# Four edits around norm boundaries, weight slabs and row loads in a six-layer fp32 kernel on one core

## What is computed

```python
for i in range(2):                                  # first block
    h = rms_norm(x, norm_mix[i]);  x = x + (dsa_moba_mixer if i == 0 else nsa_mixer)(h, ...)
    x = x + memory_cross_attention(rms_norm(x, norm_mem[i]), rms_norm(mem, norm_mem_src[i]), ...)
    x = x + swiglu(rms_norm(x, norm_ffn[i]), ffn_w_in[i], ffn_w_out[i])     # 1024 -> 2*2816 -> 1024
for i in range(4):                                  # second block
    mod = silu(c) @ ada_w[i] + ada_b[i];  sh1, sc1, g1, sh2, sc2, g2 = split(mod, 6)
    h = rmsnorm(x, mix_norm_g[i]) * (1 + sc1) + sh1
    x = x + (1 + g1) * mixer_i(h)
    h = rmsnorm(x, ffn_norm_g[i]) * (1 + sc2) + sh2
    x = x + (1 + g2) * conv_ffn(h, ff_w_up[i], ff_conv_w[i], ff_conv_b[i], ff_w_down[i])
return rmsnorm(x, final_g)
```

## Time and profile before

| what | value |
|---|---|
| median of 3 runs (lowest to highest) | 2610.83 us (2610.54 to 2617.75) |
| profiled execution | 2622.73 us |
| its span, first to last instruction | 2620.9 us |
| mean granted TensorE clock | 0.966 of full |
| PE / weight loads / DVE / ACT / POOL busy | 95% / 78% / 56% / 20% / 4% |
| weight stream | 638 slabs of 512 KB; DMA mean 173 GB/s |

### The profile page before, as it was taken

One profiled execution on the slowest core, in us unless ns is written; L12 is line 12 of the kernel. 1 busy time (PEld: TensorE's weight loads), 2 busy tenths in 40 slices (PEclk: granted clock), 3 DMA queues, 4 the chain that ended last, 5 costly groups with the idle time before them and its releaser, 6 DMA issues.

```text
span 2620.9 us, 38049 instructions
## 1 busy us (share of the span) xinstructions
PE 2484.9 (95%) x14704; PEld 2054.0 (78%) x14704; DVE 1472.4 (56%) x3034; ACT 512.1 (20%) x1297; POOL 111.1 (4%) x212
## 2 busy tenths in 40 slices
PE   7898999998898999999999899999999999999997
PEld 4465999755558998689889588898787897689897
DVE  4744787456546885333676445763845674333363
ACT  2221110024311101112211332102222101102210
POOL 0000000000000000000110001100001100000000
PEclk9879999996799999999999999999999999999999
DMA  6123456630125556535776147764227774434432
GB/s 229 67 97 141 154 209 234 217 131 1 37 104 193 209 188 247 177 121 193 281 264 243 71 163 279 279 235 162 103 97 278 283 263 155 174 123 145 152 121 97
DMA packets 122351, 453.30 MB, mean 173 GB/s; under 512 B 13776, under 2 KB 13904, under 8 KB 121680
## 3 DMA queue, kind: packets, MB, share of 16 engines
q1 hardware_dynamic: 92880, 338.24, 35.7%
q0 software_dynamic: 29312, 112.80, 12.2%
HBM read 449.93 MB, written 1.05 MB: 172 GB/s over the span
## 4 chain that ended last, share of the span: by engine, by line
PE 82%; DVE 10%; DMA 3%; ACT 3%; issue 2%; SPq 0%; POOL 0%; DVEq 0%; ACTq 0%
PE pair L517 65%; PE bank L517 16%; DMA ring<-stream_dram 2%; DVE att_s L1596 1%; DVE h L1377 1%; DVE arena L1591 1%; DVE adat L1710 1%; ACT arena L1128 1%; DVE rstd L1374 1%; DVE arena L1473 1%; ACT arena L1140 1%; DMA arena<-gmws_dram 1%; PE bank L739 0%; DMA adat<-adaw_dram 0%; DVE arena L2048 0%
## 5 line engine op out<-in xcount | busy, mean ns | idle before, releaser
L517 PE MATMUL pair<-h,ring 128*128 128x256 f32 (+1 forms) x4352 | 875.8, 363 | 24.6 <-DVE x L1404 6.8
L517 PEld LDWEIGHTS pair<-h,ring 128*128 128x128 f32 x4352 | 772.8, 191 | 123.1 <-DVE arena L1682 9.2
L517 PE MATMUL pair<-arena,ring 128*128 128x128 f32 (+1 forms) x2432 | 386.1, 319 | 12.6 <-DVE x L1404 7.5
L517 PEld LDWEIGHTS pair<-arena,ring 128*128 128x128 f32 x2432 | 352.5, 194 | 43.8 <-DVE x L1404 8.3
L517 PE MATMUL pair<-ring,h 128*128 128x512 f32 (+1 forms) x768 | 325.9, 582 | 3.0 <-DVE h L1377 3.0
L517 PE MATMUL pair<-arena 128*128 128x128 f32 (+6 forms) x2178 | 271.3, 299 | 11.8 <-ACT arena L1119 3.6
L517 PEld LDWEIGHTS pair<-ring,h 128*128 128x128 f32 x768 | 142.5, 191 | 170.6 <-issue 163.8
L517 PEld LDWEIGHTS pair<-arena 128*128 128x128 f32 (+3 forms) x2178 | 229.6, 193 | 47.9 <-issue 25.6
L1710 DVE CUSTOM_DVE_ANT_0 adat<-adat,crow,cols 128x1024 f32<-128x1024 f32 x192 | 244.0, 1277 | 22.1 <-DMA adat<-adaw_dram 21.9
L517 PE MATMUL bank<-arena 128*128 128x128 f32 (+2 forms) x1976 | 239.5, 297 | 14.7 <-ACT arena L1140 7.9
L517 PEld LDWEIGHTS bank<-arena 128*128 128x128 f32 (+2 forms) x1976 | 211.7, 191 | 39.7 <-ACT arena L1140 18.4
(11 more groups left out here) (225 smaller groups left out, 1837.4 us busy)
## 6 DMA issues: line engine op xcount, KB each, us to landing
ring<-stream_dram SPq DMA_DIRECT2D x638, 512.0 KB, 4.4
adat<-adaw_dram POOLq DMA_DIRECT2D x192, 512.0 KB, 4.4
arena<-gmrows_dram POOLq DMA_DIRECT2D x2, 2560.0 KB, 11.2
arena<-cmpw_dram POOLq DMA_DIRECT2D x1, 2112.0 KB, 8.2
x<-x_in_dram SPq DMA_DIRECT2D x2, 512.0 KB, 4.7
arena<-mem_in_dram SPq DMA_DIRECT2D x1, 1024.0 KB, 12.9
arena<-gmws_dram POOLq DMA_DIRECT2D x2, 512.0 KB, 13.2
out_dram<-h POOLq DMA_DIRECT2D x2, 512.0 KB, 3.8
```

The costliest lines, as they stand in the source:

```text
L517: return nc.tensor.matmul(out, lhsT, rhs, start=start, stop=stop)
```

## The change

Four groups of edits, all in the order and the waits; the arithmetic is the same.

1. **Bank waits.** Where `bank_free` waited for the full read of a tail group (both halves), it now waits for the add of its half 0 (`x_half`), because half 1 lies in other banks. `HALF_FREED` maps the counts.
2. **Half 1's sum of squares** moves three half-width products forward in kinds F and S (`late`: n == 0, k == 7 instead of n == 1, k == 2).
3. **DVE order.** The first pair's `up_weights` moves from ahead of `residual("memo…")` to between the last square sum of half 1 and `normalise` of half 1 (`between_halves`). `mem_source(1)` moves into `up_tiles(0)`, ahead of its third pair. The first `down_weights` of `down0` and `down1` moves behind the last gated product and its `moving_sums`.
4. **Slabs and rows.** In the first `down` pair, PE waits for all four weight sums before `one 2` instead of before `two 2`, and gives the pair's slabs back there; before, it gave them back at the start of the second pair. POOL no longer waits for the gMLP rows to land (only before the output), and their second load moves six `ada_w` tiles later.

```diff
+        HALF_FREED = {}
+        for name, source in SOURCE.items():
+            lin = PLAN[source]
+            for n in range(TAIL):
+                HALF_FREED[FREER[lin.g0 + lin.groups - TAIL + n][1]] = TAILS[name] + n + 1
...
-                pool.wait_ge(sem("gm_in"), 32 * (1 + j))
...
-            ada_tiles(ADA_T // 2 + ADA_RING, 3 * ADA_T + ADA_RING)
+            ada_tiles(ADA_T // 2 + ADA_RING, 3 * ADA_T + 3 * ADA_RING)
             gm_rows(1)
-            ada_tiles(3 * ADA_T + ADA_RING, LAYERS2 * ADA_T)
+            ada_tiles(3 * ADA_T + 3 * ADA_RING, LAYERS2 * ADA_T)
+            pool.wait_ge(sem("gm_in"), 64)
...
-                    pe.wait_ge(sem("freed_" + engine), n)
+                    if engine == "dve" and n in HALF_FREED:
+                        pe.wait_ge(sem("x_half"), HALF_FREED[n])
+                    else:
+                        pe.wait_ge(sem("freed_" + engine), n)
...
                     if not lin.head:
                         ins.then_inc(sem("down_read"), 1)
-                        summed(2)
-                    ins = product(one, 2, lambda j: own[1][:, j, :], lambda j: sums[:, 1, j, :])
+                        summed(3)
+                    ins = product(one, 2, lambda j: own[1][:, j, :], lambda j: sums[:, 1, j, :], None,
+                                  t + 2 * lin.K if not lin.head and p == 0 else None)
                     if not lin.head:
                         ins.then_inc(sem("down_read"), 1)
-                        summed(3)
...
-                        late = i == 0 and n == 1 and k == 2
+                        late = i == 0 and n == 0 and k == DK - 1
...
-                if before is not None:
-                    before()
...
                     add_squares(DK - TAIL, HALVES[i], DK - TAIL + TAIL * i + 1)
+                    if i == 1 and between_halves is not None:
+                        between_halves()
                     normalise(norm, gain, i)
...
                 for t in range(1, FT):
+                    if t == 3 and early is not None:
+                        early()
...
-                down_weights(f"down{i}")
                 gated(FT - 1)
-                for _ in range(3):
+                for _ in range(4):
                     down_weights(f"down{i}")
...
-                residual(f"memo{i}", f"ffn{i}", col(f"norm_ffn{i}", 0, DK), before=lambda: up_weights(i))
+                residual(f"memo{i}", f"ffn{i}", col(f"norm_ffn{i}", 0, DK), between_halves=lambda: up_weights(i))
...
-                mem_source(1)
-                up_tiles(0)
+                up_tiles(0, lambda: mem_source(1))
```

More of the change, by code:

```diff
@@ L1384, in normalise, with residual @@
                     ins.then_inc(sem("out_ready"), 1)
-            def residual(name, norm, gain, gate=None, between=None, ebuf=None, before=None):
+            def residual(name, norm, gain, gate=None, between=None, ebuf=None, between_halves=None):
                 lin = PLAN[name]
@@ L1631, in attention, with up_tiles @@
                         between(i - first)
-            def up_tiles(i):
+            def up_tiles(i, early=None):
                 lin = PLAN[f"up{i}"]
```

## The result

| | before | after |
|---|---|---|
| first measurement, one chip | 2612.2 us median of 4 (2610.5 to 2617.8) | 2580.1 us median of 4 (2578.4 to 2582.9) |
| second, another chip | 2616.6 us median of 10 (2612.0 to 2623.8) | 2579.8 us median of 5 (2570.5 to 2582.9) |
| profiled execution, span | 2620.9 us, clock 0.966 | 2577.8 us, clock 0.974 |

The ratio is 0.9868 [0.9846, 0.9891] in the first measurement and 0.9852 [0.9829, 0.9875] in the second. The changed kernel is faster, and 2580 lies in the range of 2563 to 2588. The spans of the two profiled executions are 43.1 us apart, the medians 32.1 and 36.8.

A forecast was written before the change was run, and what follows sets the result against it. PE was taken as the bound almost everywhere, so gains come only where it idles or runs at low clock. Terms summed to 40.3 us; 38 taken from the 2610.8 median gave 2573, with an 8-in-10 range of 2563 to 2588.

The forecast's parts named there:

- the median of the runs is 12 lower: Whole kernel: median 12 below the profiled execution, partly low-clock stretches, so 38 instead of 40.3 taken off 2610.8.
- Bank waits at `memo`, 7.5 and 6.0: At `memo` in both layers: 7.5 us of PE idle saved, and 6.0 of low clock if the clock stays up.
- The rival that the clock does not come back: Gaps at `memo` and in the convolution go but clock terms are missing: 28 to 30 gained, 2582; chance 0.17.
- `up0`'s head, 3.4: From tail's end to moving product in `up0`: 17.3 us becomes layer 1's 13.9, gain 3.4, at least 0.7.
- The sums' cost ahead of the reciprocal: In `up1`, moved sums before half 1's reciprocal use up the earlier root: gain 0, loss 0.
- `memk`, `cup`: Half 1's sum runs sooner: 1.1 us each at `memk0`, `memk1`; 1.4 at `cup1`, `cup2`; 0.7 at `cup0`, `cup3`.
- Heads of `down`, 2.3: At `down` heads, without the weight sum ahead, moving sums end at least 1.2 us sooner; twice, 2.3.
- Slabs, 6.6: First `down` pair: earlier release lets the third pair's last slab land 3.8 us sooner; all 6.6 of waits go.
- Rows, 7.5: Convolution of layer 2: PE's 5.50 us wait and 2.0 of low clock go, 7.5 saved, bounds 0 and 8.
- PE does not stop: Convolution of layer 2: buffered tiles carry PE to 2008.4, the next tile comes at 2005.3.
- Cost 0 at t = 3: `mem_source` at t = 3 takes 2.2 us of DVE, but costs 0, with 1.5 as the bound.

The follow-up runs named there:

- the norms edit: Kernel before with only the bank waits on `x_half` and half 1's sum seven products into half 0: 2606.4 us median of 6, ratio 0.9956.

## Why the prediction was right, and where it was off

**The total.** Forecast 2573, measured 2580. The gain of 38 agrees with the medians over more runs: 54 runs of before have a median of 2617.5, nine of after 2579.8. The mechanism and the size of the gain were right; the seven us are in the base. The step that failed is "the median of the runs is 12 lower, and part of that may be low-clock stretches that these runs don't have". I used it to take 2 off the gain, when some 7 of the 12 were a median of three runs that had come out low.

That 38 fits so closely is partly luck. With the terms as the traces below have them (13.8, 1.1, 2.0, 2.6, 2.0, 1.6, 7.8 and 6.7 in the order of this section) the sum is 37.6: 40.3 was too much by `up0`, `down0` and the rows, too little by the slabs, and the 2 taken off for another reason happened to cover the rest.

**Bank waits at `memo`, 7.5 and 6.0.** Right: 7.0 and 6.8 with the clock in the first pair of traces, 13.8 where the sum had 13.5. The rival that the clock does not come back fell in all nine executions without the gap.

**`up0`'s head, 3.4.** Right for the first pair of traces (17.3 to 13.7), wrong as a forecast of runs. In the second execution of before the same stretch took 14.8 (270.60 to 285.38), so 1.1 remains. The rest was the low clock of one execution, which the prediction's own comparison with layer 1 showed and which I then booked in full. The sums' cost ahead of the reciprocal was right: 6.81 to 6.62, gain 0.2.

**`memk`, `cup`.** 1.0, 1.3 and 0.7 for 1.1, 1.4 and 0.7: the reading of which input comes last at half 1's sum carried.

**Heads of `down`, 2.3.** The waits of 1.17 are gone in both. In `down0` about 0.7 was lost again: a modulation tile issued at 422.10 landed after 8.4, DVE stood 3.20 for it, and PE 0.70 for the sum behind. The early release is the cause, since without it that tile lands after 3.4 to 3.6; that the five slabs take its share of the DMA engines is the likely way and not shown. The prediction had moved the slabs into a stretch that it read in `cdown0`, and did not ask what POOL has under way in `down0`.

**Slabs, 6.6.** Right that the release decides; undoing it cost 8.2, and 7.8 by waits. DVE's wait for the third pair's slabs in `down0` fell from 7.90 to 3.10. But 6.6 was one execution's figure: without the edit these waits were 4.4 to 6.9 in five executions.

**Rows, 7.5.** 6.7 in the first pair (8.3 in the last line of the table, less 1.6 that `cdown2`'s slabs bring). "PE does not stop" held in four of the five executions that have this edit whole; in the first of after it stopped for 1.25. The failed step is the landing of the tile behind the rows: 19.5 after the rows' issue (1955.98 to 1975.49) where the prediction had 15.5, and 16.7 to 18.2 in the other four. The margin of 3.0 was sized rightly and used up.

**`mem_source`.** Cost 0 at t = 3 was right: nothing waits there in any execution.

The Trainium skill, "DMA: Bandwidth & Descriptors" (Queues, rings and completion order), has each engine serve its queues in turn. The late tiles of `down0` and of the convolution are in line with it: 8.4 and 13.1 to land, beside a median of 4.6 for such a tile in the DMA part of the page of after.

## What to carry to other kernels

Read which input of the next step comes last, not which wait is longest: of the 14.2 us of waits for adds outside `memo`, the norms edit alone gained 7.6 (twice 1.0, 1.5 and 1.3), since the squares and the normalised tiles stood behind them; in the whole change 5.0, since the moved sums take 1.3 of each 1.5 back. Price a low clock by how often it follows such a gap over several executions, and take no term from a stretch that one execution alone shows. A buffer given back a product earlier can be worth as much as moved work, as long as what it lets start does not collide with a transfer that is already due. Measure buffers in time and not in tiles: the same three tiles lasted 11.4 us at one place of a stage and 15.2 at another.

## What was unexpected of the hardware

The same stretch with the same work of PE differs by up to 5.7 us between executions of these kernels (by 2.3 between the two of after), with the clock of a 20 us window at 0.83 in one execution of before and 1.00 in the other.

Behind the gaps of 1.92 the clock was low in 2 of 10 cases (20 passes in 3.94 instead of 2.50); behind the shorter halts at the heads, 0.7 to 1.4, in none of nine executions.

The first tile of 512 KB behind the 3 MB of rows and weights, with both in their new place and no wait, landed 10.3 to 10.5 us after its issue in three executions, 11.9 in a fourth and 13.1 in a fifth.

The load of ACT's table takes 1.28, and the next operation starts 0.01 to 0.02 behind it (257.13 + 1.28, then a square root at 258.42). The Trainium skill, "ScalarE: Activation LUTs" (What ACT_TABLE_LOAD costs), adds a drain of 1.38 to each switch; no such time stands in these traces: where work is waiting, the load starts 0.02 behind the operation ahead of it and the next one 0.01 to 0.02 behind the load, and all 45 loads of a trace take 1.28.
